# Down product and last norm inside the gate and up program

## The reference, cut to what matters

```
h = silu(hf @ w_ffn_gate) * (hf @ w_ffn_up)      # 1056 x 2816
y = h @ w_ffn_down                               # 1056 x 1024
out = x1 + rms_norm(y, norm_ffn_post)            # y * rsqrt(mean(y*y) + 1e-6) * gain
```

## Time and profile before

| | us |
|---|---|
| median of 3 runs | 1947.58 (1945.81 to 1949.18) |
| profiled execution | 1949.53 |
| its span | 1947.7 |
| PE busy | 1804.1 |
| DVE busy | 918.4 |
| ACT busy | 573.0 |
| POOL busy | 250.2 |

### The profile page before, as it was taken

One profiled execution on the slowest core, in us unless ns is written; L12 is line 12 of the kernel. 1 busy time (PEld: TensorE's weight loads), 2 busy tenths in 40 slices (PEclk: granted clock), 3 DMA queues, 4 the chain that ended last, 5 costly groups with the idle time before them and its releaser, 6 DMA issues. The chain is left out here.

```text
span 1947.7 us, 35078 instructions
## 1 busy us (share of the span) xinstructions
PE 1804.1 (93%) x13281; PEld 1600.3 (82%) x13281; DVE 918.4 (47%) x1845; ACT 573.0 (29%) x1185; POOL 250.2 (13%) x550
## 2 busy tenths in 40 slices
PE   7799999899886999999989999999999998999995
PEld 7789998776554767676767889999999998999995
DVE  4423332125434767777656553333333332655566
ACT  4100000223223656565656520000000001333334
POOL 3000014500511313232230000000000000000001
PEclk9999999999896989999999999999999999999998
DMA  5425956736999030211002221111111110111114
GB/s 149 158 80 141 239 151 115 230 112 214 315 296 206 2 94 6 61 39 68 21 9 80 90 79 43 49 48 43 43 44 53 43 43 22 45 43 40 41 47 190
DMA packets 157370, 184.65 MB, mean 95 GB/s; under 512 B 23673, under 2 KB 120360, under 8 KB 157186
## 3 DMA queue, kind: packets, MB, share of 16 engines
q1 hardware_dynamic: 132802, 143.89, 24.4%
q0 software_dynamic: 11040, 30.77, 5.8%
q10 hardware_dynamic: 13408, 8.42, 2.0%
HBM read 152.82 MB, written 34.38 MB: 96 GB/s over the span
## 5 line engine op out<-in xcount | busy, mean ns | idle before, releaser
L184 PE MATMUL psum<-hf_hi,gu_hi 128*128 128x352 f32 x1056 | 340.8, 323 | 0.7 <-DVE gu_lo L2515 0.7
L185 PE MATMUL psum<-hf_lo,gu_hi 128*128 128x352 f32 x1056 | 338.5, 321 | 0.0
L186 PE MATMUL psum<-hf_hi,gu_lo 128*128 128x352 f32 x1056 | 338.2, 320 | 0.0
L184 PEld LDWEIGHTS psum<-hf_hi,gu_hi 128*128 128x128 f32 x1056 | 198.1, 188 | 1.0 <-DVE gu_lo L2515 0.9
L185 PEld LDWEIGHTS psum<-hf_lo,gu_hi 128*128 128x128 f32 x1056 | 198.4, 188 | 0.0
L186 PEld LDWEIGHTS psum<-hf_hi,gu_lo 128*128 128x128 f32 x1056 | 197.9, 187 | 0.0
L184 PE MATMUL psum<-h_hi,down_hi 128*128 128x352 f32 x528 | 173.8, 329 | 18.9 <-DVE h_lo L2745 18.9
L184 PE MATMUL psum<-x_hi,w_hi 128*128 128x352 f32 x528 | 172.8, 327 | 9.6 <-DVE w_lo L632 4.9
L2015 ACT ACTIVATE probs<-psum,neg_max 128x640 f32<-128x640 f32 (+7 forms) x192 | 138.0, 719 | 121.6 <-DVE neg_max L2152 118.1
L185 PE MATMUL psum<-x_lo,w_hi 128*128 128x352 f32 x528 | 172.2, 326 | 0.0
L186 PE MATMUL psum<-x_hi,w_lo 128*128 128x352 f32 x528 | 172.1, 326 | 0.0
(11 more groups left out here) (369 smaller groups left out, 3198.3 us busy)
## 6 DMA issues: line engine op xcount, KB each, us to landing
fox_ring<-in_cache_fox_kv SPq DMA_DIRECT2D x128, 256.0 KB, 6.0
zT<-z_stage SPq DMA_DIRECT2D x22, 528.0 KB, 2.9
w_ring<-in_w_in POOLq DMA_DIRECT2D x22, 512.0 KB, 5.3
gu_ring<-in_w_ffn_gate SPq DMA_DIRECT2D x22, 512.0 KB, 3.9
gu_ring<-in_w_ffn_up SPq DMA_DIRECT2D x22, 512.0 KB, 3.9
down_ring<-in_w_ffn_down SPq DMA_DIRECT2D x44, 256.0 KB, 2.7
nsa_page<-in_cache_nsa_kv POOLq DMA_DIRECT2D x64, 128.0 KB, 6.3
out<-nat SPq DMA_DIRECT2D x12, 512.0 KB
```

The costliest lines, as they stand in the source:

```text
L184: nc.tensor.matmul(dst, w_hi, x_hi, start=start, stop=False)
L185: nc.tensor.matmul(dst, w_hi, x_lo, start=False, stop=False)
L186: return nc.tensor.matmul(dst, w_lo, x_hi, start=False, stop=stop)
```

## The change

`build_e` and `build_f` are gone; what they did stands in `build_d`, behind the loop of gate and up, on each engine, with three `Steps` semaphores (EA for ACT, EV for DVE, EP for PE) and no loops: all 44 groups are written out.

- The down tiles have their own SBUF, except the split of `hT` (`h_parts`), the squares and their sum, which lie over the gate/up ring. SP loads the first two groups of down weights behind the last gate/up load; the nine x1 loads follow the load of group 3.
- The banks rotate by six from half to half over all eight (`down_bank`).
- At the end of a half ACT alone empties the banks: it squares the output (`square_out`) and copies it to `yT` times the gain, which is now one number per partition (`out_of`). DVE adds the squares of the half up at step 2 of the next one (`sum_squares`).
- `turn_out(t, ks)` is one transpose for each k in ks, from `yT` into the bank pair of tile t (6-7, 0-1, 2-3, 4-5, and again). At the end PE sums the squares over partitions with products by a column of ones into nine cells of bank 7 (`add_up`), ACT takes one root for all tiles, DVE one reciprocal. Per token tile PE transposes eight blocks and DVE does one step: PSUM times 1/root plus x1, into `y_out`, which lies over `hT`. GpSimd does nothing there.
- The gain of the last norm is loaded with the other gains at the kernel's start, by one more DMA on GpSimd's queue.

```diff
+def down_bank(half, c, b):
+    return (6 * half + 3 * c + b + 6) % 8
 # SP, behind the gate/up loop
+                for g in range(DOWN_GROUPS):
+                    half, step = divmod(g, DOWN_STEPS)
+                    if g >= 2:
+                        EV.wait(sp, ("w_lo", g - 2))
+                    sp.dma_start(down_ring[:, g % 2], WD[:, FG * step:FG * step + FG, half * 256:half * 256 + 256]).then_inc(down_loaded[g % 2], 16)
+                    if g == 3:
+                        sp.wait_ge(gu_done[1], FT)
+                        for t in range(QT):
+                            sp.dma_start(x1[:, t, :], x1_dram[t * P:t * P + P, :]).then_inc(x1_loaded, 16)
+                        sp.dma_start(x1_last[0:S, :], x1_dram[T:N, :]).then_inc(x1_loaded, 16)
+                for t in range(QT + 1):
+                    EV.wait(sp, ("y", t))
+                    sp.dma_start(outputs[t], y_out[0:rows_of(t), t, :]).then_inc(y_stored, 16)
 # PE
+                for g in range(DOWN_GROUPS):
+                    half, step = divmod(g, DOWN_STEPS)
+                    EV.wait(pe, ("w_lo", g))
+                    for q in range(FG):
+                        f = FG * step + q
+                        EV.wait(pe, ("h_lo", g, q))
+                        if g == 0 and q == 0:
+                            pe.wait_ge(silu_ready, FT)
+                        for c in range(2):
+                            for b in range(3):
+                                if f == 0 and half and (c, b) in ((0, 2), (1, 0)):
+                                    EA.wait(pe, ("out", half - 1, 0))
+                                if f == 0 and (c, b) == (1, 2):
+                                    if half:
+                                        EA.wait(pe, ("out", half - 1, 1))
+                                    else:
+                                        pe.wait_ge(h_ready, FT)
+                                tok, col = slice(b * NB, (b + 1) * NB), slice(c * P, (c + 1) * P)
+                                last = product(nc, psum[:, down_bank(half, c, b), 0:NB], down_hi[:, g % 2, q, col], down_lo[:, g % 2, q, col],
+                                               h_parts[q][:, 0, tok], h_parts[q][:, 1, tok], f == 0, f == FT - 1)
+                            if c == 0 and f == FT - 1:
+                                EP.done(last, ("first", half))
+                        EP.done(last, ("used", g, q))
+                turn_out(0, range(KD - 2))
+                EV.wait(pe, ("sum", HALVES - 1, 0))
+                add_up(sums, False)
+                EA.wait(pe, ("square", HALVES - 1, 1))
+                EP.done(add_up(sq[:, 1, :], True), "totals")
+                EA.wait(pe, "rooted_s")
+                EP.done(turn_out(0, range(KD - 2, KD)), ("turned", 0))
+                for t in range(1, QT + 1):
+                    if t >= 4:
+                        EV.wait(pe, ("y", t - 4))
+                    EP.done(turn_out(t, range(KD)), ("turned", t))
 # ACT
+                def h_high(g, q):
+                    if g:
+                        EP.wait(act, ("used", g - 1, q))
+                    else:
+                        act.wait_ge((gu_split[1], gu_done[1])[q], FT)
...
+                def square_out(half, c):
+                    EP.wait(act, ("first", half) if c == 0 else ("used", half * DOWN_STEPS + DOWN_STEPS - 1, FG - 1))
...
+                h_high(0, 0)
+                h_high(0, 1)
+                for half in range(HALVES):
+                    for step in range(1, DOWN_STEPS):
+                        for q in range(FG):
+                            h_high(half * DOWN_STEPS + step, q)
+                    if half + 1 < HALVES:
+                        for c in range(2):
+                            h_high((half + 1) * DOWN_STEPS, c)
+                            square_out(half, c)
+                            out_of(half, c)
+                EA.done(nc.scalar.activation(spare[:, :], eps[:, :], ACT.Sqrt), "table")
+                for c in range(2):
+                    square_out(HALVES - 1, c)
+                for c in range(2):
+                    out_of(HALVES - 1, c)
+                EP.wait(act, "totals")
+                EA.done(nc.scalar.activation(e_root[:, 0:QT], psum[:, 7, TOTALS][:, 0:QT], ACT.Sqrt, bias=eps[:, 0:1], scale=1.0 / D), "rooted")
...
 # DVE; split_down(g) waits for its load and for ("used", g - 2, 1)
+                split_down(0)
+                h_low(0, 0)
                 gated(FT - 1)
+                h_low(0, 1)
+                for g in range(1, DOWN_GROUPS):
+                    half, step = divmod(g, DOWN_STEPS)
+                    split_down(g)
+                    for q in range(FG):
+                        h_low(g, q)
+                    if half and step == 2:
+                        for c in range(2):
+                            if half > 1 or c:
+                                sum_squares(half - 1, c)
+                    if g == DOWN_GROUPS - DOWN_STEPS + 2:
+                        EA.wait(dve, ("out", HALVES - 2, 1))
+                        EV.done(nc.vector.memset(psum[:, 7, TOTALS], 0.0), "zeroed")
+                sum_squares(HALVES - 1, 0)
...
+                for t in range(QT + 1):
+                    n = rows_of(t)
+                    EP.wait(dve, ("turned", t))
+                    rest = x1[:, t, :] if t < QT else x1_last[0:S, :]
+                    EV.done(nc.vector.scalar_tensor_tensor(out=y_out[0:n, t, :], in0=pair_of(t), scalar=e_rstd[0:n, t:t + 1], in1=rest, op0=ALU.mult, op1=ALU.add), ("y", t))
```

More of the change, by code:

```diff
@@ L635, in _ @@
                 low(j)
-            dve.wait_ge(const_loaded, 16 * 4)
+            dve.wait_ge(const_loaded, 16 * 5)
             dve.wait_ge(ident_loaded, 16)
@@ new lines, in gate_up_tiles, with e_act_order @@
+    return tiles, hT, down
+HALVES = 4
+DOWN_STEPS = FT // FG
+DOWN_GROUPS = HALVES * DOWN_STEPS
+TURN_PAIRS = (6, 0, 2, 4)
+TOTALS = slice(500, 500 + QT + 1)
+def e_act_order():
+    names = [("h_hi", 0, 0), ("h_hi", 0, 1)]
+    for half in range(HALVES):
+        names += [("h_hi", half * DOWN_STEPS + step, q) for step in range(1, DOWN_STEPS) for q in range(FG)]
+        if half + 1 < HALVES:
+            names += [("h_hi", (half + 1) * DOWN_STEPS, 0), ("square", half, 0), ("out", half, 0), ("h_hi", (half + 1) * DOWN_STEPS, 1),
+                      ("square", half, 1), ("out", half, 1)]
+    return names + ["table", ("square", HALVES - 1, 0), ("square", HALVES - 1, 1), ("out", HALVES - 1, 0), ("out", HALVES - 1, 1), "rooted", "rooted_s"]
@@ new lines, in build_d @@
+def build_d(nc, a, o, env, mixT, w_o, w_o_loaded, squares, hf_hi, hf_lo, gate_up, hT, down, x1, yT):
+    outputs = [o[0][0, t * P:(t + 1) * P, :] for t in range(QT)] + [o[1].rearrange("s t d -> (s t) d")]
+    h_parts, sq, sums, down_ring, down_hi, down_lo, x1_last, e_root, e_rstd, spare = (
+        down[k] for k in ("h", "sq", "total", "ring", "w_hi", "w_lo", "x1_last", "root", "rstd", "spare"))
+    y_out = hT[:, :, :].rearrange("p f n -> p (f n)")[:, 0:(QT + 1) * D].rearrange("p (t d) -> p t d", d=D)
@@ new lines, in h_low, with sum_squares @@
+                def h_low(g, q):
+                    EA.wait(dve, ("h_hi", g, q))
+                    EV.done(nc.vector.tensor_tensor(h_parts[q][:, 1, :], hT[:, FG * (g % DOWN_STEPS) + q, :], h_parts[q][:, 0, :].bitcast(F32), ALU.subtract),
+                            ("h_lo", g, q))
+                def sum_squares(half, c):
+                    EA.wait(dve, ("square", half, c))
+                    if half == 0:
+                        EV.done(nc.vector.tensor_tensor(sums[:, :], sq[:, 0, :], sq[:, 1, :], ALU.add), ("sum", 0, 1))
+                    else:
+                        EV.wait(dve, ("sum", half - 1, 1) if c == 0 else ("sum", half, 0))
+                        EV.done(nc.vector.tensor_tensor(sums[:, :], sums[:, :], sq[:, c, :], ALU.add), ("sum", half, c))
```

238 lines of the change are left out of this document (74 added, 164 removed).

## The result

The changed kernel runs in 1931.76 us (middle of 1930.14, 1931.76 and 1933.04), the kernel before beside it in 1946.69 us (four runs, 1945.05 to 1949.18). The ratio on record is 0.9914, 95% interval 0.9896 to 0.9933: faster by 0.9% (the two middle values divided give 0.9923, inside that interval). A fourth run of the changed kernel, 2547.57 us at a mean clock of 0.649 instead of 0.967, was disturbed and is left out. A second comparison on a later occasion (four runs of the changed kernel, nine of the kernel before) gave 1928.94 against 1949.93, ratio 0.9881 [0.9865, 0.9896]. The forecast was 1918.0, a ratio of 0.985: right in sign, 11 to 14 us too good, just above the range of 1912 to 1930 in the first comparison and inside it in the second.

What follows compares the result with a forecast made beforehand. PE bounds the kernel, busy 1804.1 of 1947.7 us, so only its empty or half-speed time can be won. 7.55 + 7.45 + 5.9 - 3.8 + 12.75 - 0.3 = 29.5 us, median 1918.0; eight in ten 1912 to 1930.

Steps and rivals of the forecast that it cites:

- Part 1, the entry: Before the down product: PE's wait between last gate/up product and first down product goes, gain 7.55 us.
- forecast cover of 4 us: At the entry: x1 loads end about 1653, DVE wants the group 4 load queued behind them about 1657; nothing charged.
- Part 2, the clock: Down product: pauses of at most 1.9 us no longer bring half clock, gain 7.45 us, bounds 0 and 7.45.
- rival A: Clock falls at the new short pauses, five falls and a cold tail: 11.5 us more, 1929.5; chance 0.18.
- Part 3, the boundaries: Three boundaries between column pairs: PE idle 1.89 us each instead of 3.85, gain 5.9, range 4.4 to 7.4.
- A slot is 2.864: Down product: one f tile of 18 products takes 2.864 us, so 88 slots take 252.0 us, before and after.
- Rivals B and C: B (0.07): ACT-DVE chain 0.3 us longer in each of 88 slots, 1931 us; C (0.03): same but bigger, slower than before.
- Part 4, the sums: Down product, halves 1 to 3: DVE's sums of squares delay PE by 0.38, 1.67 and 1.75, cost 3.8 us.
- Part 5, the tail: Last down product to the end: 18.7 us instead of 31.45, gain 12.75; bounds 17 and 22.
- 9 one-column products, about 0.12 each: In the tail: PE's sums over partitions take 1.1 us per nine products, first y at T+4.85.
- up to 2: In the tail: low clock in PE's transposes would cost up to 2 us; not in the forecast sum.
- Part 6, the start: Kernel start: one more gains load on GpSimd's queue costs between 0 and 0.9 us, 0.3 taken.

Runs made afterwards that it cites:

- experiment 3: The changed kernel with five more unused ACT squares at each of the three boundaries, to lengthen PE's pause: 1938.79 us, down product 278.8.
- experiment 6: The changed kernel with 28 columns of ones instead of one in the sums over partitions at the end: 1932.2 us, tail 22.45.
- Experiment 7: The changed kernel with ACT squaring and copying bank by bank and PE going on when the first bank is free: 1922.64 us, down product 263.56.
- Experiments 1 and 5: The changed kernel with high and low parts of h in separate tiles (1929.63 us), or in one tile with 128 bytes more per part (1924.11 us).
- experiment 2: The changed kernel with the down weights moved by 128 bytes in SBUF and the h parts left alone: 1931.14 us, slot 2.907.
- experiment 9: The changed kernel with 128 bytes more per h part, squares and copies bank by bank, sums spread, one row of ones-products: 1924.92 us, ratio to before 0.9878.

## Why the prediction came out as it did

The forecast gain of 29.5 us is 17.6 between the profiles, and 15 to 21 between the medians. Its steps in order:

- **Part 1, the entry: right.** 7.55 us gone. The loop's end and the first written-out group cost nothing that PE shows. The x1 loads did use up the forecast cover of 4 us: DVE waited 0.63 for the ring load of group 4, PE for nothing.
- **Part 2, the clock: right, and shown.** 1.00 for 266.8 us with pauses of 1.65; experiment 3 brings the fall back with pauses of 4.12. In the down product rival A has nothing for it but the one fall in experiment 6. The page that spoke for A (the Trainium skill, TensorE: Matmul & The Clock Gate, A second HAM failure mode: psum-queue depth-cycling) describes small idles that make the clock swing; here nine pauses of 0.14 to 1.65 us, with the banks rotating, did not.
- **Part 3, the boundaries: mechanism right, the size 0.46 too small each.** The idle times are 0.17 and 1.65, forecast 0.19 and 1.70. But the forecast worked them out from start to start, and so measured they are 0.33 and 1.81. What I left out besides is that the products after a pause start further apart, 0.26 to 0.27 instead of 0.16. 1.4 us in all. Experiment 7 shows that ACT's list is what PE waits for: with its order changed, 5.5 us of these waits became 1.5.
- **"A slot is 2.864", carried over as it was: wrong, 3.8 us.** The sum takes 252.0 us for 88 slots from a kernel in which the parts lay elsewhere. The slot measured 2.907. Experiments 1 and 5 brought the old one back by the distance between the high and the low part alone, experiment 2 did not by moving the weights; but experiment 9 had 2.867 and 2.934 at one distance, so the distance is part of the cause and not all of it. Rivals B and C expected a longer slot too, but from a late chain of ACT and DVE. That is refuted: the subtraction ends some 0.3 us before PE wants it, and PE waits for it nowhere but at the sums. C names the right edit ("h_hi and h_lo in one tile") with the wrong mechanism and some nine times the size.
- **Part 4, the sums: right.** 0.38, 1.74 and 1.80 measured, 0.38, 1.67 and 1.75 forecast.
- **Part 5, the tail: 3.3 us too short, from two errors.** First, "9 one-column products, about 0.12 each": each is two records of about 0.12, 18 in 2.10 us. The x16 in the earlier trace rows were eight products too, and had been read as sixteen. So the 0.12, right for one record, was charged once per product and not twice: 2.2 us of add_up became 4.4, and the first y came at T+6.95 instead of T+4.85. Second, the clock fell to 0.51 from 1913.0, the first y passes started 1.61 to 1.71 us apart behind transposes at half speed, until the backlog was gone; the last began at 1926.00, 1.35 later than by the forecast spacing from 1915.05. The "up to 2" was priced and then left out of the sum. Rival A had the right place for it.
- **Part 6, the start: too small, and its remainder is open.** The early DVE step is 1.3 to 2.4 us later than before in the profiles of the changed upstream, 1.0 with the gain moved. The 3.4 us at 1133 can't be charged to that alone: the spread there from profile to profile is 6 us. The means differ by 1.8 (1134.6 and 1132.8); whether that lasts was not separated from the scatter.

So of the 11.9 us between forecast and profile, 3.8 are the slot, 1.4 the boundaries, 0.1 the sums, 3.3 the tail, and 3.35 lie upstream, mostly in scatter.

Open: why a slot depends on where the parts lie, and why the pace changes within one run; what lets the clock fall 3.7 to 6.0 us behind T, in every profile of a changed kernel, in after although PE had been busy 3.63 of the 4.00 us ahead of it; the upstream scatter.

## What to carry to other kernels

Check what a matmul's pitch is made of before multiplying it by 1584: when a change moves its operands in SBUF, the pitch may change with them, and 1.5% of it is as large as a sum of visible waits. Count records per operation in the source, not in the row, before dividing a duration by them. A pause on the path is worth shortening for two reasons, the pause and the half clock behind it (here behind every pause of 3.85 and more, behind one of 1.80, behind none of 1.67 and less), and a bound "up to 2 us" in a tail with a low-clock row of its own belongs in the sum.

## What was not expected of the hardware

- Eighteen products of 128x352 took 2.907 us with high and low part 4224 bytes apart, 2.867 at 4352, 2.864 at 8448; in experiment 9 the pace went between 2.867 and 2.934 within one run at 4352, with ACT and DVE at the same points of the slot.
- A float32 product by one column of ones shows as two matmul records of 0.117 us.
- In the down product half clock followed the only pause of 1.80 us, and none of the pauses of 1.67 and less.
- In the tail the clock fell although PE had been busy 3.63 of the 4.00 us ahead of it, and it fell too with 28-column products and with dense ones between the one-column ones.
